# Hybrid Hyena and pooling layer on one core: input pieces split and consumed one by one, a new division of labour between ScalarE and VectorE, and other quarter counts in the signal stage

## What is computed

```python
mod = silu(c) @ w_ada + b_ada;  shift, scale, gate = split(mod, 3)
u = x * (1 + scale) + shift
proj = u @ w_in + b_in                       # 24 tiles of 128 channels
hy_streams, hy_gate, pool_in, pool_gate = split(proj)
# A: Hyena. short conv over 3 tokens, then twice z = g * (long_conv(z, k) + z * bias), g = x1, x2,
#    long convs of 2L points by FFT; filters k from a small sine network times a decay window
# B: pooling. centred means over 2/4/8/16 tokens, minus the token, a 128x128 map per group
y = concat(y_hyena * silu(hy_gate), y_pool * silu(pool_gate))
out = layer_norm(ALPHA * x + gate * (y @ w_out + b_out))
```

## Time and profile before

| | us |
|---|---|
| median of three executions | 1202.82 |
| their range | 1201.72 to 1208.78 |
| the profiled execution, its own time | 1207.8 |
| its span (first to last instruction) | 1206.0 |
| TensorE busy in the span | 1097.2 (91%) |
| VectorE busy | 861.8 (71%) |
| ScalarE busy | 568.7 (47%) |
| mean granted TensorE clock | 0.962 of full |

### The profile page before, as it was taken

The page is one execution under the profiler, slowest core; times in us unless marked ns, Lnnn a source line. Parts: engine busy times, 40 slices in busy tenths (PEclk is TensorE's granted clock), DMA queues, the critical chain, the costliest instruction groups (busy, mean ns, idle before and its releaser), DMA issues. The chain is left out here.

```text
span 1206.0 us, 14196 instructions
## 1 busy us (share of the span) xinstructions
PE 1097.2 (91%) x4928; PEld 846.4 (70%) x4928; DVE 861.8 (71%) x1105; ACT 568.7 (47%) x745; POOL 12.5 (1%) x32
## 2 busy tenths in 40 slices
PE   3799579999999999988999999898999669999995
PEld 1278458888888877666887876666787457888884
DVE  6699794555545545539999746554999967888878
ACT  4078642444535353526777634343786763221210
POOL 0001000000000000000000000000000000000000
PEclk8789889999999999989999999999999979999998
DMA  9959963677675525578999668778799999566321
GB/s 340 312 178 306 335 235 109 193 233 244 227 256 175 190 97 200 191 229 244 278 274 283 194 201 263 239 234 243 228 295 271 285 328 313 163 201 197 134 88 53
DMA packets 155132, 273.24 MB, mean 227 GB/s; under 512 B 11503, under 2 KB 49519, under 8 KB 153396
## 3 DMA queue, kind: packets, MB, share of 16 engines
q1 hardware_dynamic: 151605, 266.74, 68.7%
q0 software_dynamic: 3168, 5.51, 2.0%
q10 hardware_dynamic: 288, 0.08, 0.0%
HBM read 178.95 MB, written 98.57 MB: 230 GB/s over the span
## 5 line engine op out<-in xcount | busy, mean ns | idle before, releaser
L177 PE MATMUL u_pp<-uh_uhi,prj_whi 128*128 128x512 f32 x768 | 311.7, 406 | 21.8 <-DMA p_first<-in_t_kfirst 10.3
L178 PE MATMUL u_pp<-u_ulo,prj_whi 128*128 128x512 f32 x768 | 307.3, 400 | 0.0
L179 PE MATMUL u_pp<-uh_uhi,prj_wlo 128*128 128x512 f32 x768 | 306.9, 400 | 0.0
L177 PEld LDWEIGHTS u_pp<-uh_uhi,prj_whi 128*128 128x128 f32 x768 | 147.3, 192 | 64.1 <-issue 20.9
L179 PEld LDWEIGHTS u_pp<-uh_uhi,prj_wlo 128*128 128x128 f32 x768 | 147.4, 192 | 34.8
L178 PEld LDWEIGHTS u_pp<-u_ulo,prj_whi 128*128 128x128 f32 x768 | 147.6, 192 | 33.0
L1255 DVE TENSOR_TENSOR p_alo<-p_a,p_ahi 128x1024 fp32r<-128x1024 f32 x32 | 39.2, 1226 | 101.7 <-ACT p_ahi L1196 101.7
L1196 ACT ACTIVATE p_ahi<-p_a 128x1024 fp32r<-128x1024 f32 x32 | 34.0, 1061 | 126.2 <-PE p_ps L179 121.2
L2195 ACT ACTIVATE p_sm<-p_mv,p_eps 128x1 f32<-128x1 f32 x16 | 4.7, 294 | 107.8 <-DVE p_mv L2286 107.8
L559 PE MATMUL fs_s<-fs_khi,flt_tab 64*128 64x512 f32 x256 | 51.4, 423 | 4.2 <-ACT prj_cv L603 2.2
L598 ACT ACTIVATE fs_khi<-fs_k 128x1024 fp32r<-128x1024 f32 x32 | 33.9, 1060 | 40.5 <-DVE fs_k L575 40.5
(11 more groups left out here) (210 smaller groups left out, 2110.5 us busy)
## 6 DMA issues: line engine op xcount, KB each, us to landing
p_a<-kseq SPq DMA_DIRECT2D x32, 512.0 KB, 4.3
kfreq<-p_out SPq DMA_DIRECT2D x32, 512.0 KB, 5.2
xseq<-p_xo SPq DMA_DIRECT2D x32, 512.0 KB, 7.8
p_k_re<-kfreq SPq DMA_DIRECT2D x64, 256.0 KB, 5.7
p_k_im<-kfreq SPq DMA_DIRECT2D x64, 256.0 KB, 5.0
bseq<-p_out SPq DMA_DIRECT2D x32, 512.0 KB, 5.6
prj_ws<-in_t_win SPq DMA_DIRECT2D x24, 512.0 KB
kseq<-prj_row SPq DMA_DIRECT2D x22, 512.0 KB, 4.4
```

The source lines that it names most:

```text
L177: nc.tensor.matmul(out, w[0], m[0], start=start, stop=False, skip_group_check=True)
L178: nc.tensor.matmul(out, w[0], m[1], start=False, stop=False, skip_group_check=True)
L179: return nc.tensor.matmul(out, w[1], m[0], start=False, stop=stop, skip_group_check=True)
```

## The change

Six edits that belong together:

- Buffers 4 to 7 of the input become four `pairs`, allocated outside the stages. `front` uses them as `arg`, `turn`, `h` and `wraw`; `values_and_filters` uses them as `a` and `out`. The loads of pieces 4 to 7 move from the start of `values_and_filters` into `filter_stage1`, one behind each of the stores 24 to 27.
- TensorE's wait for the tables moves from ahead of everything to ahead of `unit(0)`, and its wait for the input goes by piece: each quarter waits only for the piece it reads.
- Of pieces 4 to 15 the odd ones are formed on ScalarE (`form_u_act`, L727: two ACTIVATE of 128x512 with scale and bias from columns, in place), right ahead of the high part of the even piece before; the even ones on VectorE, two pieces ahead of the low part made next.
- In steps -3 and -2 ScalarE reads out the finished chunk (`to_row`) ahead of the pieces, no longer behind them.
- In the signal stage the quarters are spread: 4 4 3 3 3 3 3 2 3 3 2 3 3 2 3 2 2 4, still 52.
- In the tail, inv(2) stands behind product(0) instead of ahead of it.

```diff
@@ filter_stage1, sync
                     pj.load_consts(sp)
+                if N - 8 <= n < N - 4:
+                    pj.load_x(sp, n - (N - 12))
@@ Projection.__init__
         self.xt += [self.side, self.cv[:, 2 * CH:4 * CH].rearrange("p (a b) -> p a b", a=2)]
+        self.xt += xin.pairs
@@ values_and_filters
-        a = [s.sb(f"a{b}", [P, 2, DH]) for b in range(2)]
+        a, out = pj.xt[4:6], pj.xt[6:8]
-        out = [s.sb(f"out{b}", [P, 2, DH]) for b in range(2)]
-        pj.xt += [*a, *out]
-        by_act = ()
+        by_act = range(5, 16, 2)
@@ sync
-            for m in range(4, 8):
-                pj.load_x(sp, m)
             pl.load(sp)
@@ tensor
-            pe.wait_ge(tabs_in, 32)
             for step in range(plan.lo, S):
+                if step == 1:
+                    pe.wait_ge(tabs_in, 32)
...
                 for q, part in early:
-                    if q < 4 and part == 0:
-                        for m in range(4 * q, 4 * q + 4):
-                            pe.wait_ge(pj.ulo_done[m % 8], m // 8 + 1)
-                pj.quarter_chunks(pe, early)
+                    if q < 4:
+                        m = 4 * q + part
+                        pe.wait_ge(pj.ulo_done[m % 8], m // 8 + 1)
+                    pj.quarter_chunks(pe, [(q, part)])
@@ scalar
+                if step in form_at and plan.due(plan.out, step) is not None:
+                    first_row(act)
+                    pj.to_row(act, plan.due(plan.out, step))
                 if step in form_at:
                     for m in form_at[step]:
-                        if m in by_act:
-                            pj.form_u_act(act, m)
+                        if m + 1 in by_act:
+                            pj.form_u_act(act, m + 1)
                         pj.high_u(act, m)
@@ vector
                 if step in form_at:
                     for m in form_at[step]:
-                        if m >= 4 and m not in by_act:
-                            pj.form_u(dve, m)
-                        if m >= 1:
-                            pj.low_u(dve, m - 1)
-                if step == plan.lo + 4:
-                    pj.low_u(dve, 15)
+                        if 4 <= m + 2 < 16 and m + 2 not in by_act:
+                            pj.form_u(dve, m + 2)
+                        pj.low_u(dve, m)
@@ inverse_and_output, tensor
-            if step + 2 < GS:
+            if 1 <= step and step + 2 < GS:
                 inv(step + 2)
...
             product(step, range(0, 4), False, True).then_inc(mm_done[r], 1)
+            if step == 0:
+                inv(2)
@@ encoder_layer
-                (-1, 17, [4, 4, 4, 4, 0, 4, 4, 4, 0, 4, 4, 4, 0, 4, 0, 4, 0, 4]),
+                (-1, 17, [4, 4, 3, 3, 3, 3, 3, 2, 3, 3, 2, 3, 3, 2, 3, 2, 2, 4]),
+                    w.pairs = [w.sb(f"pair{b}", [P, 2, DH]) for b in range(4)]
```

More of the change, by code:

```diff
@@ L291, in load_tab, with front @@
         pool.dma_start(self.tab[m % 3][:, :, :, :], tabs["w1f"][self.group(m), :, :, :, :]).then_inc(self.tab_in[m % 3], 16)
-def front(nc, t, fl, tabs, scale1, shift, rows):
+def front(nc, t, fl, tabs, scale1, shift, rows, pairs):
     MAGIC = 1.5 * 2.0 ** 23
@@ L308, in front @@
         cols = s.sb("cols", [P, 28])
-        arg = s.sb("arg", [P, 2, CH])
-        turn = s.sb("turn", [P, 2, CH])
-        h = s.sb("h", [P, 2, CH])
+        arg, turn, h, wraw = pairs
         wa = s.sb("wa", [P, KT, 3 * D])
         acc = s.sb("acc", [P, 2 * D])
-        wraw = s.sb("wraw", [P, 2, DH])
         c_silu = s.sb("c_silu", [P, KT])
@@ L1187, in _ @@
                     tn.turn(pe, turned, 3)
-                pj.quarter_chunks(pe, late)
+                for q, part in late:
+                    if q < 4:
+                        m = 4 * q + part
+                        pe.wait_ge(pj.ulo_done[m % 8], m // 8 + 1)
+                    pj.quarter_chunks(pe, [(q, part)])
         @block.scalar
@@ L1203, in evac, with first_row @@
                 nc.scalar.activation(out[n % 2][:, 0, :], ps[n % 2][:, 0, :], ACT.Copy).then_inc(even_out[n % 2], 1)
+            def first_row(act):
+                act.wait_ge(pj.consts, 2 * 16)
+                pj.filter_stored(act, (0, 1))
+                act.wait_ge(pj.pad_set, 2)
             for step in range(plan.lo, S):
@@ L1227, in _ @@
                 q = plan.due(plan.out, step)
-                if q is not None:
-                    if q == 0:
-                        act.wait_ge(pj.consts, 2 * 16)
-                        pj.filter_stored(act, (0, 1))
-                        act.wait_ge(pj.pad_set, 2)
+                if q is not None and step not in form_at:
                     if q < 16:
@@ L2360, in encoder_layer @@
                     w.ring = [w.sb(f"xt{b}", [P, 2, CH]) for b in range(2)]
+                    w.pairs = [w.sb(f"pair{b}", [P, 2, DH]) for b in range(4)]
                     fl = Filters(nc, f)
-                    front(nc, t, fl, tabs, scale1, shift, rows)
+                    front(nc, t, fl, tabs, scale1, shift, rows, w.pairs)
                     pj = Projection(nc, t, u, w, scale1, shift)
```

## The result

The changed kernel took 1199.35 us in the median of 20 executions (1194.68 to 1203.41), the kernel before 1206.26 us in 20 beside it (1201.72 to 1213.6): ratio 0.9948, interval 0.9934 to 0.9961, so 6.3 us won (4.7 to 8.0; the two medians differ by 6.9). That is clear of zero, and inside the 1% (12 us) that the prediction took for what a measurement can tell. The forecast was 1193.4, with 9.4 us won. Of the 5.95 us between forecast and time, 3.4 us lie in the base: the three executions of the kernel before, from which the forecast started, had a median 3.4 us under that of the 20, which begin with the same three. The other 2.5 to 3.1 us are gain that didn't come.

The account below looks back on a forecast made before the run. TensorE was taken to bound nearly everything, so only its waits and half-clock stretches could pay. Input part 6.0, signal stage 3.9, tail -0.5: 9.4 us off the median 1202.8 gave 1193.4, range 1185.5 to 1199.0.

Parts of the forecast that it names:

- the wait for the weight tile: Input stage: w_high(1) needs a load now asked for closer to its use; 0.5 us added (0 to 2).
- the form on ScalarE: Input stage: one piece's form on ScalarE takes 1.3 us, between 1.14 and 1.6; six of them.
- d: Delay of the filter stage by the four more loads: 3.0 us, between 0.7 and 5.2.
- A loss forecast behind unit 0: Input stage: a half-clock stretch of TensorE behind its idle, 1.5 us lost, leaving net 6.0 won.
- The idle before unit 0: End of the input stage: TensorE idles 2.5 us, as the new chain through load_a is late.
- The signal stage: Spread quarters: 4.4 us of waits go, 1.0 comes back in switching, 0.5 won at stage end; 3.9 won.
- The tail: product(0) starts sooner, but TensorE waits about 2.7 us before pooled(2), perhaps then at half clock; 0.5 us lost.
- The DMA and ScalarE take it back: Rival, filter and input stages: d 5.2, w_high waits 2 us, form 1.6; 3.9 us won, 1198.9; chance 0.12.
- Slower: Rival, input stage: TensorE fed piece by piece isn't granted the full clock; 5.8 us slower, 1208.6; chance 0.05.
- The signal edit does nothing: Rival, signal stage: a new wait takes the old one's place; 5.5 us won, 1197.3; chance 0.08.
- More is won: Rival: all uncertain terms end well, with no new half clock; 15.8 us won, 1187.0; chance 0.25.
- the prediction's rule from 1.64 and 2.15 us: TensorE's clock: idle of 2.15 us was followed by a half-clock stretch, idle of 1.64 was not.

Follow-up runs that it names:

- experiment 4: The kernel after with the loads of pieces 4 to 7 back at the start of values_and_filters: ratio 0.9938 to the kernel before.
- experiment 5: The kernel after with weight tile 0, pieces 0 to 7 and the constants loaded at the very start of filter_stage1: 0.9886 to the kernel before.
- Experiment 6: As experiment 5, with weight tile 1 also asked for ahead of pieces 8 to 15: ratio 0.9866 to the kernel before.
- experiment 8: The kernel after with all forms on VectorE, none on ScalarE: ratio 0.9912 to the kernel before.
- experiment 1: The kernel before with only the signal stage's new quarter counts: ratio 0.9971 to the kernel before, 3.5 us won.
- the second comparison: The kernel after measured once more, unchanged, against the kernel before: ratio 0.9953.

## Why the prediction was right or wrong

Two steps failed. The sum was set against too low a base (3.4 us), and in the input stage the wait for the weight tile, put at 0.5 us, was 2.08 (with the form on ScalarE, put 0.1 too low six times, this made the input stretch 2.1 us longer than forecast); d was 0.9 too small. A loss forecast behind unit 0 (1.5 us) didn't come, so that the input part missed by no more is partly luck. The mechanism was otherwise as forecast: TensorE begins with the first piece, the signal stage's waits go, the tail gives nothing.

- **The base (3.4 of the 5.95 us).** The sum was set against a median of three executions, 1202.8. Twenty gave 1206.3. The prediction had two values to choose from, this median and its profiled execution, 5.0 us above it, which it couldn't place. It took the median of three; the profiled one, 1207.8, was the more typical of the two (the medians of before in the later comparisons were 1205.6 to 1209.1).
- **The filter stage, d.** Predicted 3.0 in a range of 0.7 to 5.2; it was 3.9 in the first pair of profiles, 4.3 by the means. That the four loads delay the stage is shown by experiment 4 (26.99 us without them); the term was 0.9 to 1.3 us too small. The split into free room and a store in flight was an argument that no run separates. The waits of the read-outs for stores grew by 5.3 us, past the 5 us that the prediction had named as a sign of being wrong. What it overlooked was the larger point, that in the same trace the start of the stage was free (DMA share 0.04 from 57 to 63 us and 0.00 from 63 to 69): experiment 5.
- **The form on ScalarE.** Predicted 1.3 a piece, measured 1.41 from its start to the next (154.76 to 156.17). Over six that is 0.7 us on ScalarE's chain. The estimate from the Trainium skill's formula (ScalarE: Activation LUTs, What ACT_TABLE_LOAD costs) was 2 x 0.71 = 1.4, and the trace agrees.
- **The weight tile.** Predicted 0.5 of wait, it was 2.08. This is the term that was mis-sized most: ScalarE's chain took 28.7 us from the first high part to the end of the last instead of 26.5, and the wait reached TensorE as 3.65 us and a stretch at 1.2 GHz. Experiment 6 took 2.5 us off the input stretch by removing it. The load's place behind pieces 12 to 15 was in the text; that each of those waits for a buffer, so that the tile's load waits for the low part of piece 7, was not drawn out. In after that low part ends at 163.96, the tile's load is issued at 164.40, and ScalarE's wait for it ends at 171.43.
- **The idle before unit 0.** Predicted 2.5 us and a half-clock stretch worth 1.5; it was 0.64 and no such stretch. The load chain came as predicted in its length (w_low(1) at 181.03, low(0) ending at 190.10: 9.1 against 9.4), but TensorE, late through the tile, arrived late as well. Behind the first high part the operand was ready at 39.1 us (forecast 37.2) and TensorE at 38.6 (forecast 34.7). So the forecast loss of 1.5 us didn't come there; a stretch at 1.2 GHz lay ahead of it instead, from 176.3 to 179.8. With it the input part stood at -8.6 + 4.3 = 4.3 us by the means instead of 6.0, 3.9 by measurement.
- **The signal stage.** Predicted 3.9. The stretch shrank by 5.4 in the first pair, 5.0 by the means. The waits went as the prediction had it, and the last store's issue ended 3.3 us sooner against unit 0, beside a forecast of 4.4 - 1.0 = 3.4 (520.42 - 190.24 against 525.05 - 191.53). The rest is the stage end: the next stage began 5.0 us behind that issue instead of 7.1, where the prediction had let the end give 0.5. By measurement the edit alone is worth 3.5 and 3.7 us, less than the stretch's 4.6 to 6.2 in these kernels; both intervals are wide enough to hold 5, so whether a part is lost later is open.
- **The tail.** Predicted -0.5, measured nothing: pooled(2) waits longer for VectorE's sum (0.87 and 0.71 in the two profiles of after instead of 0.27), the way that was forecast but not by the 2.7 us, and product(0) took a new wait of 2.08 that the text didn't name.
- **The rivals.** *The DMA and ScalarE take it back* named the two terms that did fail, d and the weight tile (it gave 3.9 us won). *Slower*, TensorE at half clock when fed by pieces, is out: it stood at 0.50 up to 159.3 and then had 1.00 for 13.4 us on such food. There TensorE had a backlog and no gap; in experiment 8 it did stop before the pieces and had 1.00 all the same. The Trainium skill's pattern (TensorE: Matmul & The Clock Gate, A second HAM failure mode), short idles between groups that make the clock swing, is not what these traces show. *The signal edit does nothing* is out by experiment 1. Of *More is won* the missing half clock and more than its 0.6 at the signal stage's end came, but d and the weight tile went the other way.
- **The sum.** Parts measured alone are 3.9 + 3.5 + 0 = 7.4; together 6.3, 5.6 in the second comparison, a difference that the intervals don't separate from none. In the profiles the front takes 2.9 of what the changed stages give. That the front's length goes mostly with the kernel, and that the kernel with all forms on VectorE had a short front in both profiles and was 2.7 to 4 us faster than after in spite of a longer input stage, points to the front as the place of the missing gain. It is not shown: one of six kernels changed its group, and the middle varies by more than the difference. The kernel with the loads back even speaks against it: its front was 3.7 and 3.2 us shorter than that of after, its filter and input stretches together 0.2 and 1.0 us shorter, and yet it measured 0.9938 and 0.9953 beside 0.9948 and 0.9953; its tail was 2.3 and 3.9 us longer in the same profiles. The place of the missing gain stays open.

## What to carry to other kernels

Before a load is put between the last stores of a stage, look where the DMA engines are idle and the buffer is already free: here four loads cost 3.7 us at the end of the stage, all nine cost nothing that can be seen at its start, and moving them was worth about as much as the whole change (7.4 beside 6.3 us). In a queue that runs in order, follow each load back through every wait that stands ahead of it, since one late weight tile stopped three engines in turn. Splitting work between two engines pays by what the slower of the two still has, so look at it again after each wait that goes: six forms on the other engine shortened the stretch by 0.1 to 1.0 us while a load was late, four by 3.7 when none was.

## What the runs showed that was not expected

- Stages that the change doesn't touch move by more than its parts are worth. Front: 54.9 to 58.8 us over 18 profiles, in two groups (54.9 to 56.0 and 57.0 to 58.8); in the pair compared above the difference is when its weights land and when the clock comes back. Middle: 434.0 to 441.8 us at the same work. Tail: 229.1 to 233.0 us.
- TensorE's gate product, 32 matmuls of 128x512 with one column of weights, took 15.3 to 16.8 us, in the two profiles looked at its first part at 1.2 GHz, though it had no gap.
- A wait of 3.65 us was followed by a stretch at 1.2 GHz (0.52 from 176.3 to 179.8), waits of 0.64 (after, unit 0) and 1.3 (experiment 6, unit 0) were not. In after an idle of 1.79 before 525.40 was not followed by one either (1.00 from 526 to 536), one of 1.84 before 540.43 was (0.64 in the mean from 540.4 to 545). So the length of the idle alone doesn't tell, as the prediction's rule from 1.64 and 2.15 us had it.

```profile
531.30:545.00 13.70, 11.82 (x42) 8.92 (x43) 11.03 (x16) 5.76 (x8) 0.00 (x0) 0.88 1.05 265
```
